# Sixteen-head attention: value projection one pair ahead, out projection begun at pair 6; latent attention's two value products together; squares of x through four banks

## The chip, the cores and the metric

One Trainium2 chip, one of its cores. The metric is the device time of one execution in microseconds (us), taken as the median of several runs. The five instruction queues of the core are TensorE (PE; its weight loads are PEld), VectorE (DVE), ScalarE (ACT), GpSimd (POOL) and SyncE (SP, which only issues loads here).

## What is computed

The reference is two transformer blocks on 512 tokens of width 1024, all in float32. Cut to what the change touches:

```python
# layer 0: latent attention, 8 heads of 128 + 64 rotary, values of 128
h = rms_norm(x, attn_pre_g[0]); a = h @ w_a; cq, ckv, kr = split(a)
q = rms_norm(cq, g_q) @ w_uq;   kv = rms_norm(ckv, g_kv) @ w_ukv
o = softmax(mask(q @ k.T * scale)) @ v;   x = x + rms_norm(o @ w_o, post_g)
x = x + rms_norm(swiglu(rms_norm(x, ffn_pre_g)), ffn_post_g)
# layer 1: attention of 16 heads of 64, with a relative bias table
k, v = rms_norm(x, g_src) @ w_kv;   q = rms_norm(x, attn_pre_g[1]) @ w_q
o = softmax(q @ k.T * 0.125 + bias) @ v;  x = x + rms_norm(o @ w_o, post_g)
...
# the second block (sparse attention, convolution, feed-forward) follows; the change does not touch it
```

## The kernel before

**Units of weights.** Every weight matrix is cut into units of 128 x 1024 values, 307 in all, consumed strictly in one order. Each goes through the same line: SP loads it into one of two `raw` buffers (`load_units`), ACT rounds it into a high part (`round_unit`, L380), POOL subtracts to get the low part (`low_units`, L385), and PE uses both (`next_unit` waits for the low part). One block of a product is three matmuls of 512 columns: high weight times high activation (L401), high times low (L402), low times high (L403); `project` does eight blocks, 24 matmuls, with one unit. Rounded units sit in two slots, `whi0/wlo0` and `whi1/wlo1`, taken in turn; a few units at stage borders have slots of their own (`OWN_AT`), numbered by distance from the first unit of a stage (`FIRST`). A slot is free when the projection that read it is done, and `round_unit` waits for that. Nothing schedules the queues: each engine's program is written out by hand, and the place of each `round_unit` call among ACT's other work is part of that text.

**The latent stage** (`latents_pe`, `latents_act`, `latents_dve`) projects x into five tiles (`("a", 0)` to `("a", 4)`), while ACT squares the eight tiles of x (`square_tile`, L517) through two banks of PSUM, and DVE adds them up (`add_square`, L1049), interleaved with the rotary tables (`dve_table`). PE sums over partitions inside projection 2 (`latent_sums_pe`) and spreads the inverse root inside projection 3 at block 2 (`spread_tokens_pe`, L1040).

**Latent attention** (`mla_pe`, `mla_act`, `mla_dve`) does four pairs of heads. At the end of pair p, PE does the value product of head 0 (`mla_times_v_pe`, L898), the two transposes of the next pair's values (`mla_values_pe`, L793), then the product of head 1.

**Attention of sixteen heads** (`b_pe`, `b_act`, `b_dve`) does eight pairs. For pair p+1 three units are needed, in the order v, k, q: units 92, 93, 94 for pair 0, 95, 96, 97 for pair 1, and so on to 115; units 116 to 123 are the out projection. The join before it (`b_first_pe`) already does v0, k0, q0, v1 and k1 (units 92 to 96). In pair p PE does the scores (`pair_scores_pe`, L1347), projects v and k of pair p+1, transposes the values (`b_values_pe`, L1403), transposes the probabilities (`pair_transposes_pe`, L1369), projects q of pair p+1, and does the value product (`pair_times_v_pe`, L1384). ACT, in pair p: the exponents (`act_exp`, L450), one `round_unit`, the copy of the values (`b_values_act`, L1408), six copies of transposed probabilities (`pair_spread_act`, L1377), two more `round_unit` (one in pair 0). DVE: the row minima of the scores (L1355), the scaling of projections (`dve_scale`, L514) and the normalising of the probabilities (`dve_normalise`, L456 and L465).

**The out projection** (`out_pe`, `out_act`, `out_dve`) is eight output tiles of eight blocks. Block k needs head pair k's output. Tile 0 is begun in the last pair, with seven of its blocks.

Of the kernel before, what the change touches and what calls it, by code (L numbers as in the profile page):

```python
# [12 lines left out]
P = 128  # L13
# [197 lines left out]
def build(nc, x_in, pos_in, stream, gains_in, consts_in, rel_in, w1_in, out):  # L211
# [115 lines left out]

    X_PIECES = (0, 1, 2, 4, 6)
    turn = {}
    FIRST = {"F0": 26, "B": 92, "F1": 124, "C": 190}  # L330
    OWN_AT = {"F0": (72, 80, 64), "B": (0, 8, 16), "F1": (48, 56, 36), "C": (0, 8, 16)}
    slot, before, last_in = [], [], {}
    for u in range(n_units):
        own = [(n, i) for n in FIRST for i, d in enumerate(((-4, 0), (-3, 1), (3,))) if u - FIRST[n] in d]
# [11 lines left out]
    def own_slot_free(e, u):  # L346

        for n, b in FIRST.items():
            i = {-4: 1, -3: 3, 3: 5}.get(u - b)
# [235 lines left out]

    def latent_sums_pe(e, name, key, src):
        e.wait_ge(*formed.at(key))
        token_sums_pe(e, R_BANK[name], src, True, True).then_inc(*summed.done((name, "tokens")))

    def latents_pe(e):  # L590
# [16 lines left out]
        project(e, 3, hh, hl, ("a", 3), between={2: lambda: spread_tokens_pe(e, 4, "x", 48)})  # L607
# [27 lines left out]
    def latents_act(e):  # L635
# [61 lines left out]
    def latents_dve(e):  # L697
# [9 lines left out]
        for k in range(1, KD):  # L707
            add_square(e, "x", k, bank[6:8])
# [202 lines left out]
    def mla_pe(e):  # L911
# [10 lines left out]
        for p in range(NA):  # L922
# [5 lines left out]
            else:  # L928
                u = next_unit(e)
                e.wait_ge(*low.at(("A", p - 1, 1)))  # L930
                out_blocks_pe(e, u, 0, (0, 1, 2))
# [8 lines left out]
            mla_times_v_pe(e, p, 0)  # L940
            if more:
                mla_values_pe(e, p + 1, 0)
                mla_values_pe(e, p + 1, 1)
            else:
                out_blocks_pe(e, u, 0, (5,))
            mla_times_v_pe(e, p, 1)
        return u

    def mla_act(e):
# [14 lines left out]
        for p in range(NA):  # L964
            more = p + 1 < NA
            if p:
                mla_out_act(e, p - 1, 1)
# [10 lines left out]
            mla_out_act(e, p, 0)  # L978
            if more:
                mla_values_act(e, p + 1)  # L980
        mla_out_act(e, NA - 1, 1)
# [98 lines left out]
    def out_pe(e, key, u, done):  # L1080

        last = ("A", NA - 1, 1) if key == "oA" else ("B", PAIRS_B - 1)
        us = (u, next_unit(e))
        out_blocks_pe(e, us[1], 1, (0, 1, 2))
        e.wait_ge(*low.at(last))
        for i, k in enumerate((done, 3)):
            out_blocks_pe(e, us[i], i, range(k, KD)).then_inc(*proj.done((key, i), ("unit", us[i])))
        for m in range(2, KD):
# [6 lines left out]
    def out_act(e, key):  # L1095
        for m in range(KD - 1):
            round_unit(e)
# [300 lines left out]

    def b_values_pe(e, p):

        e.wait_ge(*evicted.at(("vB", p) if p else ("kB", 1)))
        for t in range(QT):
            mm = e.transpose(bank[5 if p else 7][:, t * P:(t + 1) * P], vtmpB[:, t * P:(t + 1) * P], ident)  # L1403
# [759 lines left out]
```

## Time and profile before

| | |
|---|---|
| median of 3 runs | 1985.27 us (1985.1 to 1985.39) |
| the profiled execution, its own time | 1981.76 us |
| its span | 1980.0 us |
| PE busy | 1938.3 us, 98% of the span |
| POOL, ACT, DVE busy | 732.4, 722.6, 958.4 us |
| granted clock of TensorE, mean | 0.991 |

A busy share of 98% says that little can be won by making anything but PE wait less, and much can be lost by making PE wait. The timeline gives each instruction's start and length. Lengths of matmuls are modelled and overlap: successive matmuls of 512 columns start 0.23 us apart at full clock although each reads 0.39. So a stretch of PE's work is measured here from start to start.

### The profile page before, as it was taken

What the parts mean: (1) busy time and instruction counts of PE and PEld (TensorE: products, weight loads), DVE (VectorE), ACT (ScalarE), POOL (GpSimd) and SP (SyncE); (2) the same over time, 40 slices, a digit from 0 to 9 for tenths busy, and PEclk for the clock granted to TensorE, in tenths of its full rate; (3) what the DMA queues carried; (4) which work ended last, traced back from release to release, by engine and by line L of the source; (5) the groups of instructions that cost most, each with busy time, mean ns of one, the idle gap of its engine ahead of it and who ended that gap; (6) DMA issues with size and microseconds to landing.
All of it is one profiled execution on the core that took longest, in us unless ns stands there. A gap on an engine that the chain in (4) does not pass through costs nothing.

```text
span 1980.0 us, 22714 instructions
## 1 busy us (share of the span) xinstructions
PE 1938.3 (98%) x9094; PEld 1565.8 (79%) x9094; DVE 958.4 (48%) x1649; ACT 722.6 (36%) x1172; POOL 732.4 (37%) x309
## 2 busy tenths in 40 slices
PE   8999999999998999999999999899999999999998
PEld 7777888888886777888888888788677888888887
DVE  7563564441036445264444005894665765555202
ACT  6554422222244444332222224223654343333221
POOL 2333244444441222524444452342112444444442
PEclk9999999999999999999999999999899999999999
DMA  4412122332231222312233231321111222322222
GB/s 161 167 60 79 55 95 98 99 101 96 96 107 54 86 95 75 117 44 96 99 99 100 97 107 65 127 96 55 42 33 54 96 86 97 100 100 97 96 96 86
DMA packets 52152, 178.60 MB, mean 90 GB/s; under 512 B 5680, under 2 KB 5824, under 8 KB 51792
## 3 DMA queue, kind: packets, MB, share of 16 engines
q1 hardware_dynamic: 45776, 164.09, 25.1%
q10 hardware_dynamic: 6272, 13.07, 1.9%
q8 instruction: 72, 1.18, 0.2%
q14 instruction: 32, 0.26, 0.0%
HBM read 175.00 MB, written 6.33 MB: 92 GB/s over the span
## 4 chain that ended last, share of the span: by engine, by line
PE 87%; DVE 6%; ACT 3%; issue 2%; DMA 1%; POOL 1%; SPq 0%; DVEq 0%; ACTq 0%
PE bank L401 24%; PE bank L403 24%; PE bank L402 24%; PE bank L1384 2%; PE bank L1369 1%; PE bank L1137 1%; PE bank L1131 1%; PE bank L1132 1%; PE bank L1770 1%; PE bank L843 1%; PE bank L1347 1%; DVE tmp L1049 1%; PE bank L1040 1%; POOL wlo L385 1%; DMA raw<-stream 1%
## 5 line engine op out<-in xcount | busy, mean ns | idle before, releaser
L385 POOL TENSOR_TENSOR wlo<-raw,whi 128x1024 fp32r<-128x1024 f32 x285 | 684.6, 2403 | 1203.5 <-ACT whi L380 1203.4
L380 ACT ACTIVATE whi<-raw 128x1024 fp32r<-128x1024 f32 x287 | 304.1, 1060 | 851.6 <-PE bank L403 828.2
L401 PE MATMUL bank<-hh,whi 128*128 128x512 f32 x1384 | 545.1, 394 | 7.6 <-POOL wlo L385 6.3
L402 PE MATMUL bank<-hl,whi 128*128 128x512 f32 x1384 | 540.8, 391 | 0.0
L403 PE MATMUL bank<-hh,wlo 128*128 128x512 f32 x1384 | 540.7, 391 | 0.0
L401 PEld LDWEIGHTS bank<-hh,whi 128*128 128x128 f32 x1384 | 261.6, 189 | 71.4 <-issue 14.5
L403 PEld LDWEIGHTS bank<-hh,wlo 128*128 128x128 f32 x1384 | 261.1, 189 | 55.3
L402 PEld LDWEIGHTS bank<-hl,whi 128*128 128x128 f32 x1384 | 261.5, 189 | 53.2 <-issue 0.2
L514 DVE TENSOR_TENSOR tmp<-bank,rs 128x512 f32<-128x512 f32 x154 | 105.3, 689 | 237.8 <-PE bank L403 223.5
L401 PE MATMUL bank<-fh,whi 128*128 128x512 f32 x496 | 192.9, 389 | 0.0
L402 PE MATMUL bank<-fl,whi 128*128 128x512 f32 x496 | 192.9, 389 | 0.0
L403 PE MATMUL bank<-fh,wlo 128*128 128x512 f32 x496 | 192.9, 389 | 0.0
L1312 DVE TENSOR_TENSOR tmp<-tmp,tmp 128x512 f32<-128x512 f32 x44 | 99.0, 2249 | 49.9 <-ACT tmp L1267 49.5
L1326 DVE COPY y<-bank 128x512 f32<-128x512 f32 x16 | 11.0, 688 | 206.7 <-PE bank L403 206.7
L403 PEld LDWEIGHTS bank<-fh,wlo 128*128 128x128 f32 x496 | 93.1, 188 | 19.5
L402 PEld LDWEIGHTS bank<-fl,whi 128*128 128x128 f32 x496 | 93.1, 188 | 19.4
L401 PEld LDWEIGHTS bank<-fh,whi 128*128 128x128 f32 x496 | 93.1, 188 | 19.1
L1696 DVE SCALAR_TENSOR_TENSOR bank<-zpad,gn,bank 128x512 f32<-128x512 f32 x112 | 74.8, 749 | 0.0
L401 PE MATMUL bank<-oh,whi 128*128 128x512 f32 x160 | 63.7, 398 | 1.6 <-POOL wlo L385 1.5
L402 PE MATMUL bank<-ol,whi 128*128 128x512 f32 x160 | 62.3, 390 | 0.0
L403 PE MATMUL bank<-oh,wlo 128*128 128x512 f32 x160 | 62.3, 389 | 0.0
L1049 DVE TENSOR_TENSOR tmp<-tmp,bank 128x512 f32<-128x512 f32 x72 | 49.1, 683 | 24.9 <-ACT bank L517 23.5
(281 smaller groups left out, 2424.8 us busy)
## 6 DMA issues: line engine op xcount, KB each, us to landing
raw<-stream SPq DMA_DIRECT2D x307, 512.0 KB, 3.4
bias_scratch<-rel_scratch ACTq DMA_DIRECT2D x1, 4096.0 KB, 18.9
biasB<-bias_scratch ACTq DMA_DIRECT2D x16, 256.0 KB, 2.8
w<-w_in ACTq DMA_DIRECT2D x2, 1024.0 KB, 5.9
out<-y ACTq DMA_DIRECT2D x8, 256.0 KB, 2.1
x<-x_in SPq DMA_DIRECT2D x3, 512.0 KB, 8.9
x<-x_in SPq DMA_DIRECT2D x2, 256.0 KB, 5.5
cst<-consts_in SPq DMA_DIRECT2D x1, 448.0 KB, 4.3
```

The lines of the kernel that those rows point to most:

```text
L380: e.activation(slot[u][0][:, :], raw[u % 2][:, :], ACT.Copy).then_inc(*w_hi.done(u))
L385: e.tensor_tensor(slot[u][1][:, :], raw[u % 2][:, :], slot[u][0][:, :].bitcast(F32), ALU.subtract)\
L401: e.matmul(o, wh, h, start=first, stop=False)
L402: e.matmul(o, wh, l, start=False, stop=False)
L403: return e.matmul(o, wl, h, start=False, stop=last)
L514: e.tensor_tensor(dst, bank[bk][:, :], r[:, :], ALU.mult).then_inc(*evicted.done(key))
L843: e.matmul(bank[bk][:, c:c + W(t)], qn[b][h][:, t * P:(t + 1) * P], kn[b][h][:, 0:W(t)], start=False, stop=True, skip_group_check=True).th ...
L1040: mm = e.matmul(bank[bk][:, t * P:(t + 1) * P], stat[:, col + t:col + t + 1].to_broadcast([P, P]), ident, start=True, stop=True)
L1049: e.tensor_tensor(tmp[7][:, :], tmp[7][:, :], through[m % len(through)][:, :], ALU.add).then_inc(*formed.done((key, "sq", m)))
L1312: e.tensor_tensor(u[:, :], (bank[5] if conv else u)[:, :], g[:, :], ALU.mult).then_inc(*formed.done((key, "product", j)))
L1384: mm = e.matmul(bank[7][64 * h:64 * h + 64, k * P:T], vf(k, h), PTs[h][:, PT_AT[k]:PT_AT[k] + T - k * P], start=first and k == 0, stop=las ...
L1696: e.scalar_tensor_tensor(tmp[4][:, :] if tap == TAPS - 1 else s, zp[:, tap:tap + T], gg("dw", c * TAPS + tap), s, ALU.mult, ALU.add).then_ ...
```

## The change

It has five parts.

1. In pair p of the sixteen-head attention PE projects k and q of pair p+1 between the scores and the transposes, and v of pair **p+2** after the transposes (before: v and k, then q, all of pair p+1). In pair 0 it projects q1 there, transposes both v0 and v1, and projects v2 after. v1 is kept in `tmp7`. ACT's sequence in a pair is left as it was, but for the copies of pair 0 and one `round_unit` in pair 7, taken from the first tile of the out projection.
2. Pair 6 has no v to project, so it begins out tile 0 (five blocks); pair 7 does blocks 5 and 6 of it and seven blocks of tile 1; `out_pe` then begins tile 2. Three units are thus open together, and unit 118 gets its own slot.
3. Latent attention does both value products together, then the transposes of values.
4. Squares of x go through four banks instead of two.
5. The inverse root of x is spread at block 6 of projection 3 instead of block 2.

```diff
-    OWN_AT = {"F0": (72, 80, 64), "B": (0, 8, 16), "F1": (48, 56, 36), "C": (0, 8, 16)}
+    OWN_AT = {"F0": (72, 80, 64), "B": (0, 8, 16), "F1": (48, 56, 36, 40), "C": (0, 8, 16)}
...
+    X_THROUGH = (bank[6], bank[7], bank[3], bank[4])
...
-        project(e, 3, hh, hl, ("a", 3), between={2: lambda: spread_tokens_pe(e, 4, "x", 48)})
+        project(e, 3, hh, hl, ("a", 3), between={6: lambda: spread_tokens_pe(e, 4, "x", 48)})
...
-            square_tile(e, "x", k, x[:, k, :], bank[6:8])
+            square_tile(e, "x", k, x[:, k, :], X_THROUGH)
...
             mla_times_v_pe(e, p, 0)
+            if not more:
+                out_blocks_pe(e, u, 0, (5,))
+            mla_times_v_pe(e, p, 1)
             if more:
                 mla_values_pe(e, p + 1, 0)
                 mla_values_pe(e, p + 1, 1)
-            else:
-                out_blocks_pe(e, u, 0, (5,))
-            mla_times_v_pe(e, p, 1)
...
-    def out_pe(e, key, u, done):
...
+    def out_pe(e, key, begun, ahead):
+
+        n = len(begun)
+        u = next_unit(e)
+        out_blocks_pe(e, u, n, range(ahead))
+        e.wait_ge(*low.at(("A", NA - 1, 1) if key == "oA" else ("B", PAIRS_B - 1)))
+        for m, (um, done) in enumerate(begun + [(u, ahead)]):
+            out_blocks_pe(e, um, m, range(done, KD)).then_inc(*proj.done((key, m), ("unit", um)))
+        for m in range(n + 1, KD):
...
     def out_act(e, key):
         for m in range(KD - 1):
-            round_unit(e)
+            if m or key == "oA":
+                round_unit(e)
...
     def b_pe(e):
-            if more:
-                if p == 0:
-                    b_values_pe(e, 0)
-                else:
-                    project(e, 5, hh, hl, ("vB", p + 1))
-                if p:
-                    e.wait_ge(*stats.at(((("B", p), 1), "min", 1)))
-                    project(e, 6, hh, hl, ("kB", p + 1))
-                b_values_pe(e, p + 1)
+            if p == 0:
+                e.wait_ge(*evicted.at(("vB", 1)))
+                project(e, 5, h2h, h2l, ("qB", 1))
+                b_values_pe(e, 0)
+                e.wait_ge(*stats.at(((("B", 0), 1), "min", 1)))
+                b_values_pe(e, 1)
+                e.wait_ge(*spread.at(("vB", 0)))
+            elif more:
+                e.wait_ge(*evicted.at(("vB", p + 1)))
+                project(e, 5, hh, hl, ("kB", p + 1))
+                e.wait_ge(*stats.at(((("B", p), 1), "min", 1)))
+                project(e, 6, h2h, h2l, ("qB", p + 1))
+                e.wait_ge(*evicted.at(("kB", p + 1)))
+                b_values_pe(e, p + 1)
             else:
-                u = next_unit(e)
                 e.wait_ge(*low.at(("B", p - 1)))
-                out_blocks_pe(e, u, 0, range(6))
+                out_blocks_pe(e, u, 0, (5, 6))
+                e.wait_ge(*stats.at(((("B", p), 1), "min", 1)))
+                u1 = next_unit(e)
+                out_blocks_pe(e, u1, 1, range(4))
...
             pair_transposes_pe(e, ("B", p), probsB)
             if more:
-                e.wait_ge(*spread.at(("vB", p + 1)))
-                project(e, 5, h2h, h2l, ("qB", p + 1))
+                e.wait_ge(*(spread.at(("vB", p + 1)) if p else evicted.at(("qB", 1))))
+            if p + 2 < PAIRS_B:
+                project(e, 5, hh, hl, ("vB", p + 2))
+            elif more:
+                u = next_unit(e)
+                out_blocks_pe(e, u, 0, range(5))
             else:
-                out_blocks_pe(e, u, 0, (6,))
+                out_blocks_pe(e, u1, 1, (4, 5, 6))
...
     def b_act(e):
             if more:
                 load_bias(e, p + 1, 0)
                 load_bias(e, p + 1, 1)
-                round_unit(e)
+            round_unit(e)
+            if p == 0:
+                b_values_act(e, 0)
+            if more:
                 b_values_act(e, p + 1)
...
     def b_dve(e):
-            if more:
-                e.wait_ge(*proj.at(("vB", p + 1)))
-                if p == 0:
-                    e.wait_ge(*turned.at(("vB", 0)))
-                dve_scale(e, 5, rs[0], vtmpB[:, :], ("vB", p + 1))
+            if p and more:
+                e.wait_ge(*proj.at(("kB", p + 1)))
+                dve_scale(e, 5, rs[0], kB[nb][:, :], ("kB", p + 1))
...
```

The first place is PE in pair 1 of the sixteen-head attention, from its first projection to its value product. `whi0` and `whi1` are the two slots, `hh` the activation for k and v, `h2h` that for q; the other 23 matmuls of each projection are left out. Before:

```order
L1347 MATMUL bank3<-kB1_93,qB1_91 128x512
L401 MATMUL bank5<-hh_50,whi0_54 128x512 [waits weight_low]
L401 MATMUL bank6<-hh_50,whi1_55 128x512 [waits weight_low,statistic]
L1403 MATMUL bank5<-cst_135,vtmpB_100 128x128 [waits evicted]
L1369 MATMUL bank0<-cst_135,probsB0_96 128x128 [waits statistic,normalised,low_part]
L401 MATMUL bank5<-h2h_88,whi0_54 128x512 [waits weight_low,transposed_copied]
L1384 MATMUL bank7<-PTB0_98,vB1_95 64x512 [waits transposed_copied]
```

and in the changed kernel:

```order
L1350 MATMUL bank3<-kB1_93,qB1_91 128x512
L402 MATMUL bank5<-hh_50,whi1_55 128x512 [waits weight_low,evicted]
L402 MATMUL bank6<-h2h_88,whi0_54 128x512 [waits weight_low,statistic]
L1412 MATMUL bank5<-cst_135,vtmpB_100 128x128 [waits evicted]
L1372 MATMUL bank0<-cst_135,probsB0_96 128x128 [waits statistic,normalised,low_part]
L402 MATMUL bank5<-hh_50,whi1_55 128x512 [waits weight_low,transposed_copied]
L1387 MATMUL bank7<-PTB0_98,vB1_95 64x512 [waits transposed_copied]
```

The three projections were units 98, 99 and 100 (slots 0, 1, 0) and are now units 99, 100 and 101 (slots 1, 0, 1): one unit further in the stream, at the same three places.

The second place is ACT in the same pair 1, in the changed kernel, from the last exponent on (L451) through the two bias loads, three roundings (L381), the copy of values (L1417) and the copies of probabilities (L1380):

```order
L451 ACTIVATE probsB1_97,stat_142<-probsB1_97,stat_142 128x512 [waits statistic]
L1400 DMA biasB0_101<-bias_scratch 128x512 [waits statistic]
L1400 DMA biasB1_102<-bias_scratch 128x512 [waits statistic]
L381 ACTIVATE whi0_54<-raw0_52 128x1024 [waits projected,raw_loaded0]
L1417 ACTIVATE vB0_94<-bank5 128x512 [waits transposed]
L1380 ACTIVATE PTB0_98<-bank0 128x512 [waits transposed,mixed]
L1380 ACTIVATE PTB1_99<-bank2 128x512 [waits transposed]
L1380 ACTIVATE PTB1_99<-bank3 128x512 [waits transposed]
L1380 ACTIVATE PTB1_99<-bank7 128x256 [waits transposed]
L381 ACTIVATE whi1_55<-raw1_53 128x1024 [waits projected,raw_loaded1]
L381 ACTIVATE whi0_54<-raw0_52 128x1024 [waits projected,raw_loaded0]
```

Before, the rows are the same, in the same order (with L450, L1397, L380, L1408 and L1377 as their lines): the roundings of pair 1 are units 100, 101 and 102 in both kernels. Nothing moved here while PE moved.

The third place is PE at the end of pair 0 of latent attention (L898 the value products, L793 the transposes of values). Before:

```order
L898 MATMUL bank7<-PTB0_98,vA00_80 128x128
L793 MATMUL bank6<-cst_135,vtmpB_100 128x128 [waits evicted]
L793 MATMUL bank5<-cst_135,tmp7_131 128x128 [waits evicted]
L898 MATMUL bank1<-PTB1_99,vA01_81 128x512 [waits transposed_copied]
L898 MATMUL bank1<-PTB1_99,vA01_81 128x128
```

and in the changed kernel:

```order
L901 MATMUL bank7<-PTB0_98,vA00_80 128x128
L901 MATMUL bank1<-PTB1_99,vA01_81 128x512 [waits transposed_copied]
L901 MATMUL bank1<-PTB1_99,vA01_81 128x128
L796 MATMUL bank6<-cst_135,vtmpB_100 128x128 [waits evicted]
L796 MATMUL bank5<-cst_135,tmp7_131 128x128 [waits evicted]
```

The product of head 1 now stands between the product of head 0 and the wait for the evicted values.

## Rows read from the trace of the kernel before

**Rows 1.** Busy time by engine, then clock, DMA share, GB/s: pair 0; pairs 1 to 6.
```profile
616.00:638.00 22.00, 15.84 (x85) 10.78 (x85) 10.78 (x31) 11.43 (x27) 3.03 (x2) 0.92 0.17 61
638.00:781.00 143.00, 143.00 (x770) 109.72 (x768) 71.30 (x198) 64.08 (x156) 43.14 (x19) 1.00 0.27 89
```

**Rows 2.** Timeline of PE, pair 1: start us, length us, engine, line, what.
```profile
638.32 2.43 PE L1347 MATMUL bank<-kB,qB 64*128 64x128 f32 x16
640.68 0.50 PE L401 MATMUL bank<-hh,whi 128*128 128x512 f32 x1
...
652.13 2.35 PE L1369 MATMUL bank<-cst,probsB 128*128 128x128 f32 x20
654.24 0.48 PE L401 MATMUL bank<-h2h,whi 128*128 128x512 f32 x1
```

**Rows 3.** Timeline of ACT, pair 1: last exponent's sum, roundings, copies of probabilities.
```profile
644.70 0.19 ACT L450 ACTIVATION_READ_ACCUMULATOR probsB<-probsB,stat 128x1 f32 x1
646.51 1.06 ACT L380 ACTIVATE whi<-raw 128x1024 fp32r<-128x1024 f32 x1 [1.63 <-PE bank L403]
...
652.83 2.62 ACT L1377 ACTIVATE PTB<-bank 128x512 f32<-128x512 f32 x6
655.28 1.10 ACT L380 ACTIVATE whi<-raw 128x1024 fp32r<-128x1024 f32 x1
```

**Rows 4.** Timeline of ACT, POOL and PE: one unit from rounding to first use.
```profile
797.11 1.06 ACT L380 ACTIVATE whi<-raw 128x1024 fp32r<-128x1024 f32 x1 [5.51 <-PE bank L403]
...
798.25 2.40 POOL L385 TENSOR_TENSOR wlo<-raw,whi 128x1024 fp32r<-128x1024 f32 x1 [15.42 <-ACT whi L380]
...
800.70 0.50 PE L401 MATMUL bank<-oh,whi 128*128 128x512 f32 x1 [0.29 <-POOL wlo L385]
```

**Rows 5.** Granted clock (third number from the end) after PE's longest wait, 5.50 us.
```profile
1256.00:1258.00 2.00, 1.73 (x4) 1.47 (x5) 2.00 (x5) 0.00 (x0) 0.13 (x1) 0.50 0.44 86
1258.00:1260.00 2.00, 2.00 (x7) 1.56 (x7) 2.00 (x5) 0.69 (x2) 0.00 (x0) 0.67 0.46 184
```

**Rows 6.** Timeline of PE, pair 0, from the scores' end to the projection of q1.
```profile
618.86 0.66 PE L1403 MATMUL bank<-cst,vtmpB 128*128 128x128 f32 x4
622.18 0.66 PE L1403 MATMUL bank<-cst,vtmpB 128*128 128x128 f32 x4 [2.67 <-DVE vtmpB L514]
...
629.65 0.99 PE L1369 MATMUL bank<-cst,probsB 128*128 128x128 f32 x7 [1.84 <-DVE probsB L465]
630.39 0.48 PE L401 MATMUL bank<-h2h,whi 128*128 128x512 f32 x1
```

**Rows 7.** Timeline of DVE and POOL, pair 1: two normalisings and a low part.
```profile
647.26 3.41 DVE L465 TENSOR_SCALAR probsB<-probsB,stat 128x128 f32<-128x128 f32 x4
...
650.80 1.28 DVE L465 TENSOR_SCALAR probsB<-probsB,stat 128x128 f32<-128x128 f32 x4
...
647.65 2.48 POOL L385 TENSOR_TENSOR wlo<-raw,whi 128x1024 fp32r<-128x1024 f32 x1 [7.98 <-ACT whi L380]
```

**Rows 8.** Timeline of PE, end of pair 1 of latent attention.
```profile
117.38 0.66 PE L793 MATMUL bank<-cst,vtmpB 128*128 128x128 f32 x4 [0.75 <-DVE vtmpB L514]
...
118.47 2.32 PE L898 MATMUL bank<-PTB,vA 128*128 128x512 f32 x8
120.72 1.14 PE L838 MATMUL bank<-krope,qr 64*128 64x128 f32 x8
```

**Rows 9.** Timeline of PE and ACT, latent stage: two waits, unit 5's rounding, projection 4.
```profile
28.12 0.50 PE L401 MATMUL bank<-hh,whi 128*128 128x512 f32 x1 [0.81 <-POOL wlo L385]
...
37.83 1.16 PE L1040 MATMUL bank<-cst,stat 128*128 128x128 f32 x8 [1.69 <-DVE stat L695]
...
42.92 0.39 PE L401 MATMUL bank<-hh,whi 128*128 128x512 f32 x1
...
37.47 1.04 ACT L380 ACTIVATE whi<-raw 128x1024 fp32r<-128x1024 f32 x1
```

**Rows 10.** Timeline of DVE, pair 7: sum of the minimum that frees bank 6.
```profile
786.05 0.08 DVE L1355 DVE_READ_ACCUMULATOR2_ANT stat<- 128x1 f32 x1
```

More of the change, by code:

```diff
@@ L330, in build @@
     FIRST = {"F0": 26, "B": 92, "F1": 124, "C": 190}
-    OWN_AT = {"F0": (72, 80, 64), "B": (0, 8, 16), "F1": (48, 56, 36), "C": (0, 8, 16)}
+    OWN_AT = {"F0": (72, 80, 64), "B": (0, 8, 16), "F1": (48, 56, 36, 40), "C": (0, 8, 16)}
     slot, before, last_in = [], [], {}
     for u in range(n_units):
-        own = [(n, i) for n in FIRST for i, d in enumerate(((-4, 0), (-3, 1), (3,))) if u - FIRST[n] in d]
+        own = [(n, i) for n in FIRST for i, d in zip(range(len(OWN_AT[n])), ((-4, 0), (-3, 1), (3,), (-6,))) if u - FIRST[n] in d]
         if own:
@@ L707, in latents_dve @@
         for k in range(1, KD):
-            add_square(e, "x", k, bank[6:8])
+            add_square(e, "x", k, X_THROUGH)
             dve_table(e, next(tables))
@@ L930, in mla_pe @@
                 e.wait_ge(*low.at(("A", p - 1, 1)))
+                e.wait_ge(*spread.at(("v1", p)))
                 out_blocks_pe(e, u, 0, (0, 1, 2))
@@ L1397, in load_bias, with values_of @@
         e.dma_start(biasB[h][:, :], bias_dram[2 * p + h, :, :]).then_inc(*bias_got[h].done(p))
+    VALUES_IN = (7, 6) + (5,) * (PAIRS_B - 2)
+    def values_of(p):
+        return tmp[7] if p == 1 else vtmpB
     def b_values_pe(e, p):
-        e.wait_ge(*evicted.at(("vB", p) if p else ("kB", 1)))
+        e.wait_ge(*evicted.at(("vB", p)))
         for t in range(QT):
-            mm = e.transpose(bank[5 if p else 7][:, t * P:(t + 1) * P], vtmpB[:, t * P:(t + 1) * P], ident)
+            mm = e.transpose(bank[VALUES_IN[p]][:, t * P:(t + 1) * P], values_of(p)[:, t * P:(t + 1) * P], ident)
         mm.then_inc(*turned.done(("vB", p)))
@@ L1407, in b_values_act @@
         e.wait_ge(*turned.at(("vB", p)))
-        e.activation(vB[p % 2][:, :, :], bank[5 if p else 7][:, :].rearrange("p (k c) -> p k c", c=P), ACT.Copy).then_inc(*spread.done(("vB", p)))
+        e.activation(vB[p % 2][:, :, :], bank[VALUES_IN[p]][:, :].rearrange("p (k c) -> p k c", c=P), ACT.Copy).then_inc(*spread.done(("vB", p)))
     def b_mins_dve(e, p, h):
@@ L1501, in b_dve @@
             if more:
-                if p:
-                    e.wait_ge(*proj.at(("kB", p + 1)))
-                    dve_scale(e, 6, rs[0], kB[nb][:, :], ("kB", p + 1))
                 e.wait_ge(*proj.at(("qB", p + 1)))
-                dve_scale(e, 5, rs[0], qB[nb][:, :], ("qB", p + 1))
+                dve_scale(e, 6 if p else 5, rs[0], qB[nb][:, :], ("qB", p + 1))
+            if p + 2 < PAIRS_B:
+                e.wait_ge(*proj.at(("vB", p + 2)))
+                e.wait_ge(*turned.at(("vB", p + 1 if p else 0)))
+                dve_scale(e, 5, rs[0], vtmpB[:, :], ("vB", p + 2))
             e.wait_ge(*mixed.at(("B", p)))
```

23 lines of the change are left out of this document (7 added, 16 removed).

## The prediction

> **What bounds the kernel now.** I read the busy times by stage first. PE is the bound, and in pairs 1 to 6 of the sixteen-head attention it never rests: 143.00 us busy in 143.00 [rows 1]. Only pair 0 shows holes, 15.84 busy in 22.00. Then I read PE's timeline there, for what ends its waits, and beside it ACT's, since every projection needs a weight unit that ACT rounds and POOL completes. In pair 1 the scores start at 638.32; call that S. The first projection starts at S + 2.36, and the transposes run from 652.13 (S + 13.81) to 654.24 [rows 2]. ACT ends its exponents at about 644.79 (S + 6.47) and its copies of probabilities at 655.28, where the next rounding starts [rows 3]. The rounding at 646.51 waited for PE to free the slot, not PE for it: weights are early. From the start of a rounding to PE's first matmul with that unit is 800.70 - 797.11 = 3.59 us [rows 4]. A projection takes 24 matmuls of 0.227, 5.45 us: 630.39 + 5.45 is pair 0's product, and the two projections of pair 1 fit between 640.68 and 652.13 (2 x 5.45, plus 0.45 for the transposes of values, leaves next to nothing).
>
> **The change, part by part.** The sum is made against the profiled execution, 1981.76 us; the median of the runs, 1985.27, lies 3.5 above it, and I carry that offset over.
>
> *Pairs 1 to 6: the weights come late.* Nothing is added to PE's work: the same three projections stand at the same three places of a pair. But each uses the unit one further on, while ACT rounds the units where it did. Before, pair 1 used units 98, 99, 100; now 99, 100, 101, and ACT rounds 100 after the exponents and 101 after the copies of probabilities.
> - Unit 100, for q2, is wanted at S + 2.36 + 5.45 = S + 7.81. ACT is in its exponents until S + 6.47, so PE can start at S + 6.47 + 3.59 = S + 10.06 [rows 3, 4]. PE waits 2.25. Before, the unit in this place had been rounded in the pair before.
> - Unit 101, for v3, is wanted when the transposes are done, 2.11 after their start [rows 2]. ACT rounds it behind six copies, which themselves need the transposes; that rounding starts 655.28 - 652.13 = 3.15 after their start, and PE can use it 3.59 later, at 6.74 [rows 2 to 4]. PE waits 4.63. No slack elsewhere shortens this: transposes, copies, rounding, low part, projection are now one chain.
>
> Behind these waits on PE stand the value product and the next pair's scores, and DVE and ACT wait for those, so the pair gets longer by 6.9. In pair 6 the third user is out tile 0 (unit 116), with the same wait. Six pairs: 6 x 6.88 = **+41.3**. The bias loads, the raw loads and the second rounding at the pair's end keep their slack: unit 102 is done some 2.4 after unit 101, long before its use.
>
> *The clock.* In pairs 1 to 6 it is 1.00 now, 2.4 GHz [rows 1]. No row shows a wait of 4.6 that recurs. The nearest are the 5.50 us wait, after which the clock was 0.50, then 0.67 of full (1.2 GHz, then back), a loss of 0.5 x 1.73 + 0.33 x 2 = 1.5 us [rows 5], and pair 0, whose waits of 2.67 and 1.59 bring the mean of 22 us to 0.92 [rows 1, 6]. So a wait of 4.6 costs between 0 and 1.5; it is nearest to the 5.50, but part of the slow time may fall into the wait, so I take 1.2, six times: **+7.2** (0 to 9). For the wait of 2.25, nearer to the 1.84 of pair 0, I take 0 (0 to 9 for six).
> The Trainium skill's page TensorE: Matmul & The Clock Gate ("HAM oscillation — how this bites in real kernels") says that recurring waits between bursts throttle the array again every time, so that each burst starts cold. That speaks against this change; by it all twelve waits would pay, a rival below.
>
> *Pair 0.* From the end of the scores to the projection of q1 are 630.39 - 618.86 = 11.5 us, for 3.1 us of transposes: 8.4 of waiting [rows 6]. Now q1's projection fills the first 5.45 (unit 97 is ready), the values take 0.9, and the probabilities should be turned by about 628. Why 628: DVE scales v1 before the minima, which makes them 0.2 later than in pair 1 relative to the scores, so the exponents end near 616.5 + 6.7 = 623.2 and the second head is normalised between 625 and 627.5. The projection of v2 follows at 628 where q1's began at 630.39, with 5.45 more already done: 2.4 + 5.45 = **-7.8** (-6 to -8.4). That the second normalising may take 3.4 instead of 1.3 is the spread: one beside a low part on POOL took 3.41, one alone 1.28 [rows 7].
> The Trainium skill's SBUF — State Buffer ("Who interferes with whom") calls the port pair that DVE and GpSimd share an exclusive lock; the trace agrees. In pairs 1 to 6 that lengthens the first normalising too, but it ends by S + 11.5 and the transposes now start at S + 16, so it costs nothing there.
>
> *Pair 7 and the out projection.* PE does the same 24 + 24 + 24 matmuls of tiles 0 to 2. New is a wait for bank 6: the minimum is read at 786.05, 4.6 after that pair's scores, and blocks 5 and 6 end at 2.36 + 1.36 = 3.7, so 0.9 is lost [rows 10]. Gone are the 0.29 wait of the third tile for POOL and about a microsecond of small gaps, since more work stands between a slot's release and its next use [rows 4]: **-0.4** (-1.0 to +1.5, the latter if unit 118's low part holds up DVE).
>
> *Latent attention.* PE waits 0.75 for evicted values before their transposes, in three pairs [rows 8]. Now the product of head 1, 120.72 - 118.47 = 2.25, stands in that wait; the copies it needs are done before. Next late is the values' copy on ACT, needed only in the second half of the scores, 3 us on. 3 x 0.73 = **-2.2** (-1.5 to -2.4).
>
> *Latent stage.* With four banks ACT's squares no longer wait for DVE, so unit 3 is rounded when its slot is free and the 0.81 wait goes. The spread at block 6 comes 12 matmuls, 2.7 us, later, so its 1.69 wait goes [rows 9]. That is 2.5 at most. What is late next is unit 5 for projection 4: it is rounded at 37.47, behind the cosine and the root on ACT, which move by 0.4 at most; 37.1 + 3.59 = 40.7 against 42.92 before gives **-2.2** (-1.0 to -2.5).
>
> Sum: 41.3 + 7.2 - 7.8 - 0.4 - 2.2 - 2.2 = **+35.9**, so 1981.76 + 35.9 = 2017.7 for a profiled execution, and **2021** for the median. Least: 41.3 - 8.4 - 1.0 - 2.4 - 2.5 = +27. Most: 41.3 + 9 + 9 - 6 + 1.5 - 1.5 - 1.0 = +52.
>
> **The rivals.**
> - *A. The weights are in time; faster.* The five savings then stand alone: -12.6, 1972.7. It needs unit 100 by S + 7.8 and unit 101 by the end of the transposes, that is roundings that start by S + 4.2 and before the copies. For it speaks that every rounding in pairs 1 to 6 had to wait for a slot, not for ACT, or came early. Against it, ACT runs in written order and that order did not move. It decides from a rounding 2.3 and 4.6 earlier than I find.
> - *B. Only one of the two waits bites*, the second: +41.3 falls by 13.5, giving 2007.7. For it: the first is only 2.25, and exponents that ended 2 us sooner would hide it. Against: they are tied to the scores through DVE, unchanged.
> - *C. The clock never falls*: +35.9 - 7.2 = +28.7, 2014. For it: the waits are shorter than the 5.50.
> - *D. It falls after both waits* of each pair: +35.9 + 9 + 1.8, 2032.
>
> **How the numbers follow.** Forecast 0.60, A 0.05, B 0.07, C 0.15, D 0.11, and 0.02 for a change that moves nothing measurable. The forecast's own spread is about 5 to each side; 2008 to 2033 takes in C and D and about half of B, and leaves out A. A measurement of this kernel can tell 0.2%, 4 us, from no change. Faster by more than that only in A: 0.05; same 0.02; slower 0.93.
>
> **What would show it.** PE busy falls to about 112 in 143 us of pairs 1 to 6, a pair takes 31 to 32 us instead of 143.00 / 6 = 23.8, and the first matmul of a projection waits for POOL's low part some 12 times, 2.2 and 4.6 us long. ACT's roundings no longer wait for PE there. The clock shows about six short drops. In pair 0 the wait for the values is gone; in latent attention the 0.75 waits are gone; the spread of x's root waits for nothing. I am wrong if the low parts are there before PE asks, or if a pair still takes 24 us.

## The result: slower by 2.4%, and the profile after

The changed kernel takes 2032.12 us (median of 6 runs, 2029.99 to 2032.76). The kernel before takes 1984.35 us (median of 6 runs, 1982.75 to 1985.39). The ratio is 1.024, with a 95% interval of 1.0226 to 1.0253. The prediction was 2021 us in a range of 2008 to 2033, with 0.93 on slower: the direction and the range hold, and the time is 11 us above the forecast. It comes within 1 us of the range's upper end, and it falls on the number of rival D, 2032.

The profiled execution of the changed kernel has a span of 2031.0 us, 51.0 more than before. Its page, first the busy times, then the group of the first matmuls of a projection block with its idle time:

```profile
span 2031.0 us, 22734 instructions
...
PE 1955.8 (96%) x9094; PEld 1577.7 (78%) x9094; DVE 952.0 (47%) x1649; ACT 720.5 (35%) x1172; POOL 731.4 (36%) x309
...
L402 PE MATMUL bank<-hh,whi 128*128 128x512 f32 x1384 | 549.4, 397 | 29.0 <-POOL wlo L386 27.8
```

The same number of matmuls, 9094, keeps PE busy 17.5 us longer than before (1938.3). Where the granted clock reads 0.50, as after the wait of 4.47 in pair 1, a matmul of 512 columns has a length of 0.63 us in place of 0.39; that is what makes the busy time grow. The other 33.5 us of the 51 are idle time. The row of the page is for the activation `hh` alone; the view of PE's waits takes all of them together (total, times, longest):

```profile
PE bank L402 <- POOL wlo L386: 46.3, 16, 5.5
```

Before, that wait was 7.8 us in 5 times. Twelve of the 16 stand in pairs 1 to 6 and make 38.8 of the 46.3. By stretch (pair 0, then pairs 1 to 6 and half a pair around them; columns as in [rows 1]):

```profile
613.00:632.00 19.00, 18.75 (x106) 14.02 (x106) 11.16 (x32) 10.17 (x26) 4.76 (x2) 1.00 0.29 94
638.00:781.00 143.00, 115.14 (x536) 86.09 (x535) 46.75 (x143) 43.88 (x109) 30.45 (x13) 0.90 0.21 67
```

Against [rows 1], pair 0 has lost its holes (before, 15.84 busy in 22.00 us at a clock of 0.92). The 143 us in which PE never rested now have 115 busy, at a mean clock of 0.90, and 536 records in place of 770.

PE's timeline of pair 1 answers to [rows 2] and shows both waits. Here S, the start of the scores, is 632.58:

```profile
632.58 2.43 PE L1350 MATMUL bank<-kB,qB 64*128 64x128 f32 x16
...
642.67 0.47 PE L402 MATMUL bank<-h2h,whi 128*128 128x512 f32 x1 [2.00 <-POOL wlo L386]
648.65 2.35 PE L1372 MATMUL bank<-cst,probsB 128*128 128x128 f32 x20
655.46 0.77 PE L402 MATMUL bank<-hh,whi 128*128 128x512 f32 x1 [4.47 <-POOL wlo L386]
663.87 2.37 PE L1387 MATMUL bank<-PTB,vB 128*64 128x512 f32 x16
666.18 2.00 PE L1350 MATMUL bank<-kB,qB 64*128 64x128 f32 x14
```

Unit 100 is used at S + 10.09; the prediction had S + 10.06. Unit 101 is used 655.46 - 648.65 = 6.81 after the transposes start; the prediction had 6.74. ACT's and POOL's timelines show the two chains:

```profile
638.95 0.19 ACT L451 ACTIVATION_READ_ACCUMULATOR probsB<-probsB,stat 128x1 f32 x1
639.05 1.04 ACT L381 ACTIVATE whi<-raw 128x1024 fp32r<-128x1024 f32 x1
...
649.34 2.62 ACT L1380 ACTIVATE PTB<-bank 128x512 f32<-128x512 f32 x6
651.79 2.04 ACT L381 ACTIVATE whi<-raw 128x1024 fp32r<-128x1024 f32 x2
```

```profile
640.17 2.35 POOL L386 TENSOR_TENSOR wlo<-raw,whi 128x1024 fp32r<-128x1024 f32 x1 [10.99 <-ACT whi L381]
652.97 4.68 POOL L386 TENSOR_TENSOR wlo<-raw,whi 128x1024 fp32r<-128x1024 f32 x2 [10.45 <-ACT whi L381]
```

ACT begins the rounding of unit 100 right behind its last exponent, POOL follows, and PE waits for both. ACT no longer waits for PE there, as it did at 646.51 before [rows 3]: the slot is free and the rounding is what is late. All six pairs have the same two waits, 2.00 and 4.47.

The starts of the scores give the length of each pair. Before, each pair took 23.86 us. Now pairs 1 to 5 take 33.60, 32.27, 34.02, 34.05 and 34.04. Pair 6 takes 31.99, with 15 matmuls (3.4 us) where a projection (5.45 us) stood, so 34.04 for equal work. The waits alone make 30.74, as experiment 2 shows. The rest is the clock. Three stretches of the changed kernel (third number from the end): after the 4.47 wait of pair 1, after the 2.00 wait of pair 2 and after the 2.00 wait of pair 4:

```profile
654.00:656.00 2.00, 0.54 (x1) 0.50 (x2) 0.00 (x0) 0.00 (x0) 2.00 (x2) 0.65 0.00 0
656.00:658.00 2.00, 2.00 (x6) 1.58 (x5) 0.00 (x0) 0.00 (x0) 1.65 (x1) 0.50 0.74 250
...
676.00:678.00 2.00, 1.73 (x8) 1.47 (x9) 1.97 (x8) 0.00 (x0) 0.12 (x1) 1.00 0.38 84
678.00:680.00 2.00, 2.00 (x11) 1.65 (x10) 0.59 (x2) 0.00 (x0) 0.00 (x0) 1.00 0.46 178
...
742.00:744.00 2.00, 1.44 (x5) 1.25 (x6) 1.97 (x7) 0.00 (x0) 0.41 (x1) 0.84 0.34 49
744.00:746.00 2.00, 2.00 (x6) 1.51 (x6) 0.88 (x3) 0.00 (x0) 0.00 (x0) 0.50 0.54 213
```

At 0.50 (1.2 GHz) a window of 2 us counts 6 matmuls, at 1.00 (2.4 GHz) 11. The clock fell after all six waits of 4.47 and after four of the six waits of 2.00, those of pairs 3 to 6: ten times. In pairs 3 to 6 both falls together cost 34.04 - 30.74 = 3.3 us. In pairs 1 and 2 the one fall, after the 4.47, cost 2.86 and 1.53.

### The profile page after: what moved, and what is told of

Same layout as the page of the kernel before. It is cut to its first block, busy times and chain, and to the rows that moved or that the text cites. A ratio compares the mean times of both kernels' runs of the same rounds, so it can differ in the third digit from the quotient of the medians.

```text
span 2031.0 us, 22734 instructions
## 1 busy us (share of the span) xinstructions
PE 1955.8 (96%) x9094; PEld 1577.7 (78%) x9094; DVE 952.0 (47%) x1649; ACT 720.5 (35%) x1172; POOL 731.4 (36%) x309
## 4 chain that ended last, share of the span: by engine, by line
PE 84%; DVE 6%; ACT 5%; POOL 2%; issue 2%; DMA 1%; SPq 0%; ACTq 0%; DVEq 0%
PE bank L402 24%; PE bank L403 23%; PE bank L404 23%; POOL wlo L386 2%; PE bank L1387 2%; ACT probsB L451 1%; ACT whi L381 1%; PE bank L1140 1%; PE bank L1134 1%; PE bank L1135 1%; PE bank L1792 1%; PE bank L846 1%; PE bank L901 1%; DVE tmp L1051 1%; PE bank L1042 1%
## 5 line engine op out<-in xcount | busy, mean ns | idle before, releaser
L381 ACT ACTIVATE whi<-raw 128x1024 fp32r<-128x1024 f32 x286 | 302.3, 1061 | 809.0 <-PE bank L404 784.9
L451 ACT ACTIVATE probsB<-probsB,stat 128x128 f32<-128x128 f32 (+1 forms) x64 | 35.2, 552 | 90.8 <-DVE stat L1358 90.8
L386 POOL TENSOR_TENSOR own_lo<-raw,own_hi 128x1024 fp32r<-128x1024 f32 x21 | 50.2, 2391 | 34.4 <-ACT own_hi L381 34.3
```

The lines of the kernel that those rows point to most:

```text
L381: e.activation(slot[u][0][:, :], raw[u % 2][:, :], ACT.Copy).then_inc(*w_hi.done(u))
L386: e.tensor_tensor(slot[u][1][:, :], raw[u % 2][:, :], slot[u][0][:, :].bitcast(F32), ALU.subtract)\
L451: e.activation(r, r, ACT.Exp, scale=-1.0, bias=stat[:, st + t:st + t + 1], accum_out=stat[:, st + 4 + t:st + 5 + t]).then_inc(*expd.done(( ...
```

## The experiments

Theory: PE waits only because it uses each unit one place further on while ACT rounds where it did, and each wait brings its own fall of the clock. The rivals are given with each run.

**1. ACT one unit ahead as well.**

```diff
             if more:
                 load_bias(e, p + 1, 0)
                 load_bias(e, p + 1, 1)
-            round_unit(e)
+            if more:
+                round_unit(e)
...
             if more:
                 round_unit(e)
-                if p:
-                    round_unit(e)
+                round_unit(e)
```

> The changed kernel with one rounding of a weight unit moved on ACT: from pair 7 of the sixteen-head attention to the end of pair 0, so that ACT, too, is one unit further in pairs 1 to 6. My theory (PE waits in pairs 1 to 6 only because its projections use the unit one further on while ACT rounds as before): no wait of PE for POOL's low part is left in pairs 1 to 6, the clock stays at full there, a pair takes about 23.9 us again, and the whole time falls by about 60 us against the changed kernel, to 1970 to 1975 us, which is also 10 us under the kernel before. Rival 1 (the order of the projections itself, or the value product behind it, makes the pair longer): pairs stay over 30 us and the time stays above 2015. Rival 2 (the rounding that comes earlier at the end of pair 0 only moves the wait, because its slot is not free): waits of 2 to 5 us with the releaser ACT or POOL remain in each pair, time between 1985 and 2020.

Measured: 1971.85 us (1970.68 to 1973.04), ratio to the kernel before 0.9936 (0.9923 to 0.995). In pairs 1 to 6 no wait of PE is left in the trace. Pairs 1 to 5 take 23.86 us each, as before. From the windows view of this run, 640 to 780 us:

```profile
640.00:780.00 140.00, 139.31 (x752) 106.28 (x751) 71.97 (x203) 63.99 (x156) 43.29 (x18) 1.00 0.27 88
```

ACT's timeline of this run, at the end of pair 0, behind pair 1's exponents and behind pair 1's copies:

```profile
625.24 1.10 ACT L381 ACTIVATE whi<-raw 128x1024 fp32r<-128x1024 f32 x1
630.07 1.06 ACT L381 ACTIVATE whi<-raw 128x1024 fp32r<-128x1024 f32 x1 [3.73 <-PE bank L404]
...
640.39 1.06 ACT L381 ACTIVATE whi<-raw 128x1024 fp32r<-128x1024 f32 x1 [1.63 <-PE bank L404]
...
649.16 1.10 ACT L381 ACTIVATE whi<-raw 128x1024 fp32r<-128x1024 f32 x1
```

The row at 640.39 again waits 1.63 for PE, exactly as in [rows 3]. One `round_unit` moved 60 us (2032.1 - 1971.9). The order of the projections on PE costs nothing by itself, and both named rivals fall.

**2. The waits kept, the clock held up.**

```diff
                 e.wait_ge(*stats.at(((("B", p), 1), "min", 1)))
+                fill_clock(e, 7, 6)
                 project(e, 6, h2h, h2l, ("qB", p + 1))
...
+            if p and more:
+                fill_clock(e, 17, 5)
             if p + 2 < PAIRS_B:
                 project(e, 5, hh, hl, ("vB", p + 2))
```

> The changed kernel with matmuls that keep TensorE at work during its two waits for weights in pairs 1 to 6: 7 matmuls of 512 columns of constants (1.6 us) into bank 6 ahead of the projection of q, and 17 (3.9 us) into bank 5 ahead of the third projection; both banks are overwritten by what follows, and the results are unchanged. This parts the cost of the waits from that of the clock. Theory (each of the two waits is followed by a drop of the granted clock to half that costs about 1.65 us; 11 drops between 654 and 826 us of the changed kernel): the first matmul of each projection comes no earlier, but the clock stays at 1.00, a pair takes 23.86 + 2.0 + 4.5 + 0.3 = 30.7 us instead of 34.0, and the time is about 18 us under the changed kernel, near 2014. Rival 1 (the pair is 34 us long because of the waits and something that follows from them other than the clock, such as DVE or ACT being late): the clock stays full but the pair stays over 33 us, less than 5 us won. Rival 2 (the matmuls that fill come too late or end too late and only add to the wait): pairs of 34 to 36 us with a full clock.

The filling matmuls are of 128 columns in float32, which the trace shows as two matmuls each, not of 512 as the expectation says; their time, 1.72 and 3.96 us, is close to what is stated there. Measured: 2012.16 us (2011.39 to 2012.33), 20.0 under the changed kernel. PE's timeline in pair 1 of this run:

```profile
638.34 1.72 PE L1029 MATMUL bank<-cst 128*128 128x128 f32 x14
640.42 0.50 PE L402 MATMUL bank<-h2h,whi 128*128 128x512 f32 x1 [0.35 <-POOL wlo L386]
646.45 2.35 PE L1372 MATMUL bank<-cst,probsB 128*128 128x128 f32 x20
648.63 3.96 PE L1029 MATMUL bank<-cst 128*128 128x128 f32 x34
653.18 0.50 PE L402 MATMUL bank<-hh,whi 128*128 128x512 f32 x1 [0.59 <-POOL wlo L386]
```

The third projection again starts 653.18 - 646.45 = 6.73 after the transposes, so the weights come as late as before, but the clock is 1.00 over 140 us:

```profile
640.00:780.00 140.00, 134.35 (x800) 108.63 (x800) 46.96 (x142) 46.91 (x113) 33.33 (x15) 1.00 0.21 68
```

Pairs 1 to 4 take 30.74 to 30.76 us; pair 5 takes 31.64, because its first wait is 0.9 longer (1.27). Rivals 1 and 2 fall. So the two waits cost 30.74 - 23.86 = 6.88 us a pair, the prediction's figure, and what is above 30.74 in the changed kernel is the clock (above 28.69, this run's figure, in pair 6). Pair by pair that is 2.86, 1.53, 3.28, 3.31, 3.30 and 3.30: 17.6 us. In this run itself the pairs win 16.7, since pair 5 loses 0.9 of it again to its longer wait. The rest of the 20.0 comes from elsewhere: pair 0 begins 2.2 us earlier (611.05 for 613.22), and the stages behind pair 7, which the edit does not touch, are 1.9 us shorter.

**3. Only the first wait left.**

```diff
             round_unit(e)
+            if p and more:
+                round_unit(e)
...
             if more:
                 round_unit(e)
-                if p:
-                    round_unit(e)
```

> The changed kernel with the roundings of ACT in another place: in pairs 1 to 6 two units are rounded right after the exponents and one at the pair's end (before: one and two). The second wait (4.47 us, for the unit rounded behind six copies) should be gone, the first (2.00 us) stay. It tells what each wait costs by itself. Theory (price of the first wait 2.2 us plus its own drop of the clock, 1.65 us): a pair takes 23.9 + 2.2 + 1.65 = 27.7 us, the time is about 39 us under the changed kernel, near 1993. Rival 1 (the 2.00 wait alone does not lower the clock, as after it in pairs 1 and 2; it fell in later pairs only since both waits lie close together): pairs of 26.1, clock full, near 1983. Rival 2 (the copies of probabilities, which now stand behind two roundings, the second of which waits for PE to free the slot, become late and hold up the value product): the 4.47 wait is replaced by another behind the copies, pairs over 29 us.

Measured: 1991.65 us (1990.48 to 1993.92), ratio 1.0035 (1.0023 to 1.0047). The 4.47 waits are gone and six of 2.01 stay. Pairs 1 to 5 take 26.16, 27.74, 26.16, 27.71 and 27.72 us. Theory and rival 1 are each right in some of the pairs: without a fall the wait costs 26.16 - 23.86 = 2.30, and three of the six pairs pay some 1.55 more for one. Rival 2 falls: nothing took the place of the second wait. Two of these waits, in pairs 3 and 4 of this run, and the granted clock around them:

```profile
695.26 0.47 PE L402 MATMUL bank<-h2h,whi 128*128 128x512 f32 x1 [2.01 <-POOL wlo L386]
...
721.42 0.47 PE L402 MATMUL bank<-h2h,whi 128*128 128x512 f32 x1 [2.01 <-POOL wlo L386]
```

```profile
694.00:696.00 2.00, 0.74 (x3) 0.67 (x4) 1.97 (x3) 0.41 (x1) 2.00 (x2) 1.00 0.00 0
696.00:698.00 2.00, 2.00 (x10) 1.62 (x9) 2.00 (x3) 0.00 (x0) 1.47 (x1) 1.00 0.78 260
...
720.00:722.00 2.00, 0.58 (x3) 0.53 (x4) 1.97 (x4) 0.56 (x1) 2.00 (x2) 1.00 0.00 0
722.00:724.00 2.00, 2.00 (x7) 1.52 (x6) 2.00 (x2) 0.00 (x0) 1.61 (x1) 0.53 0.81 225
```

The waits are alike and PE does the same work around them, yet the clock stays at 1.00 after the one and falls after the other. A wait of 2 us may lower the clock or not, and these rows do not tell which.

**4. Only the second wait left empty.** The edit is the first hunk of experiment 2 alone.

> The changed kernel with constant matmuls (7 of 128 columns in float32, 1.7 us in the trace of the run that filled both waits) only ahead of the projection of q, in the first wait of pairs 1 to 6; the second wait, 4.47 us, stays empty. Results are unchanged. This is the case on which the prediction's clock term was built: both waits cost their time, and the clock falls after the second alone. Theory (each wait has its own drop, about 1.65 us): the drops after the first wait are gone, six after the second stay, a pair is 34.0 - 1.65 = 32.4 us, the time 2021 to 2024. Rival 1 (the drop after the second wait comes only because the first has already left TensorE idle: with the first filled the clock stays full throughout): pairs 30.9, time near 2013. Rival 2 (filling the first moves the drop, which comes anyway once in a pair and then lasts longer): pairs 33.5 to 34, 2029 to 2032.

Measured: 2026.2 us (2024.23 to 2030.38), ratio 1.021 (1.0193 to 1.0228), a little above the theory's 2021 to 2024. The clock no longer falls after the first wait, so each of those falls belongs to its own wait. Rival 1 falls. But the six falls after the second wait cost more than I expected of them. Pairs 1 to 5 take 33.06, 33.51, 32.25, 33.14 and 33.58 us, which is 2.32, 2.77, 1.51, 2.40 and 2.84 above 30.74; pair 6, at 30.20, is 1.51 above its 28.69 in experiment 2. Together 13.4 us, in place of 6 x 1.65 = 9.9. Rival 2 is thus partly right: in four of the pairs the clock stays low for longer. Pair 1 of the changed kernel already was such a case: its wait of 2.00 left the clock at full, and the one fall after the 4.47 cost 2.86. From the windows view of pair 1 in this run:

```profile
652.00:654.00 2.00, 0.00 (x0) 0.00 (x0) 0.00 (x0) 0.86 (x1) 2.00 (x1) 0.61 0.00 0
654.00:656.00 2.00, 1.52 (x4) 1.27 (x5) 0.00 (x0) 0.00 (x0) 2.00 (x2) 0.50 0.34 63
656.00:658.00 2.00, 2.00 (x6) 1.57 (x5) 0.00 (x0) 0.00 (x0) 0.66 (x1) 0.50 0.68 229
658.00:660.00 2.00, 2.00 (x7) 1.56 (x6) 0.00 (x0) 0.00 (x0) 0.00 (x0) 0.68 0.64 238
```

The clock is down already during the wait, and is still down 4 us after it.

**5 to 7. The latent parts on the kernel before.** Experiment 5 takes parts 3 to 5 of the change, experiment 6 part 3 alone, experiment 7 parts 4 and 5 alone. Part 3 comes with a change on ACT: the copy of head 1's output now stands behind that of head 0 and no longer in the next pair. The core of the three:

```diff
             mla_times_v_pe(e, p, 0)
+            mla_times_v_pe(e, p, 1)
             if more:
                 mla_values_pe(e, p + 1, 0)
                 mla_values_pe(e, p + 1, 1)
...
-            square_tile(e, "x", k, x[:, k, :], bank[6:8])
+            square_tile(e, "x", k, x[:, k, :], X_THROUGH)
...
-        project(e, 3, hh, hl, ("a", 3), between={2: lambda: spread_tokens_pe(e, 4, "x", 48)})
+        project(e, 3, hh, hl, ("a", 3), between={6: lambda: spread_tokens_pe(e, 4, "x", 48)})
```

> The kernel before with only the latent parts of the change: squares of x through four banks, the spread of x's inverse root at block 6, and both value products of latent attention together. The sixteen-head attention is as it was. The prediction's sum gives -2.2 for the latent stage and -2.2 for latent attention, so 1980.9 for the median. The trace of the changed kernel shows -1.84 and -3.3 for these stages, which gives 1980.1 if nothing is lost behind them; but that trace kept only 3.3 of these 5.1 by the scores of pair 0, because the clock fell for longer at 572.5 us. If such a loss comes with any shift of the start of that stage, this kernel is at 1981 to 1982; if it was chance, at 1979.5 to 1980.5. Rival: the stages behind wait for something else than PE and take the gain back, no difference (1984 to 1985).

Measured: 1978.58 us (1976.96 to 1981.39), ratio 0.9971 (0.996 to 0.9981), 6.0 us less by the medians, on the stages' 5.1. The gain is kept. This is shorter than both ranges of the expectation, and on the side of chance. The six profiled executions that run the same program up to pair 0 (the changed kernel and experiments 1 to 4 and 8) start it anywhere from 611.05 to 614.71, so the 1.9 us that the changed kernel seemed to lose there are no more than they differ by among themselves.

> The kernel before with only the latent attention of the change (both value products, then the transposes of the next values). The prediction gave -2.2 (three waits of 0.73); the traces of the changed kernel and of the run with all latent parts show -1.1 for each of three pairs, -3.3. Theory (the wait that goes is 0.75, and a further 0.35 a pair goes with the gaps around it): 3.3 less than before in the trace at the out projection, a median near 1981. Rival (the stages behind take it back, or the clock's drop near 580 us gets longer by as much): 1983 to 1984.5.

Measured: 1980.84 us (1976.91 to 1985.18), ratio 0.9983 (0.9974 to 0.9993), 3.6 us less by the medians, near the theory's 3.3. PE's timeline, end of pair 1 of latent attention in this run, which answers to [rows 8]:

```profile
114.20 4.47 PE L898 MATMUL bank<-PTB,vA 128*128 128x512 f32 x16
118.51 0.60 PE L793 MATMUL bank<-cst,vtmpB 128*128 128x128 f32 x4
...
119.48 1.14 PE L838 MATMUL bank<-krope,qr 64*128 64x128 f32 x8
```

From the first value product to the next scores it is 119.48 - 114.20 = 5.28 us. Before, it was 120.72 - 114.31 = 6.41. The recorded wait was 0.75; what went is 1.1.

> The kernel before with only the latent stage of the change (squares of x through four banks, the spread of the inverse root at block 6 of projection 3). The prediction gave -2.2 (-1.0 to -2.5); the trace of the changed kernel has -1.84 at the scores of latent attention. Theory: -1.8 in the trace at 66 us and a median near 1982.5, ratio 0.999. Rival (the earlier start is lost again at the borders of the following stages, where a wait is set by loads or by the clock): no difference.

Measured: 1982.43 us (1978.41 to 1985.89), ratio 0.9988 (0.9977 to 0.9999), 2.0 us less by the medians. The interval just leaves out 1. The trace has -2.19 at the start of latent attention's scores (63.70 for 65.89). That is one execution against one: in experiment 6, whose latent stage is the old one, these scores start at 66.91, 1.0 later than before, after a clock of 0.83 in the stretch from 12 to 20 us, where the kernel before has 1.00. The two waits of [rows 9] are gone; one of 0.3 is new, of the sums over partitions for DVE's addition of squares:

```profile
29.01 1.05 PE L1034 MATMUL bank<-cst,tmp 128*128 128x1 f32 x8 [0.28 <-DVE tmp L1051]
```

**8. A version that beats both kernels.** Experiment 1, and unit 119 rounded ahead of the square of out tile 0.

```diff
     def out_act(e, key):
         for m in range(KD - 1):
-            if m or key == "oA":
-                round_unit(e)
-            if m in (1, 2, 3):
+            round_unit(e)
+            if m in (1, 2, 3) and (key == "oA" or m > 1):
                 round_unit(e)
```

> The changed kernel with the rounding moved from pair 7 to the end of pair 0 (as in the first experiment, which gave 1971.9 and a ratio of 0.9936) and, in the out projection, unit 119 rounded ahead of the square of tile 0 instead of behind it. In that first experiment PE still waited 0.78 us for this unit at 795.41. Theory (the wait is there because the rounding stands behind a square that waits for tile 0): it goes, 0.8 us less, near 1971.1, ratio 0.9932; that is at the limit of what can be told, so the trace decides. Rival (the square comes late and the mean over the tiles with it, or the slot is not free earlier): the same 0.8 or more is lost at the next tile.

Measured: 1967.32 us (1966.95 to 1973.03), ratio 0.9918 (0.9904 to 0.9932). It is 0.8% faster than the kernel before and 3.2% faster than the changed one. Against experiment 1 the medians differ by more than the wait that was removed, but the intervals overlap, and the profiled execution here is the slowest of the six (1973.03). The stage itself decides: the trace says that the wait is gone and nothing took its place. From the start of pair 7's scores to the sums over the tiles it is 48.80 us, and 49.91 in experiment 1. ACT's timeline of this run, with the rounding now ahead of the square:

```profile
792.51 1.06 ACT L381 ACTIVATE whi<-raw 128x1024 fp32r<-128x1024 f32 x1 [6.44 <-PE bank L404]
793.48 0.62 ACT L518 ACTIVATE tmp<-y 128x512 f32<-128x512 f32 x1
```

## Why the prediction was right, and where it was 11 us short

- **The sum: predicted +35.9, measured +51.0 between the profiled executions.** For the changed kernel's profiled execution the sum gave 2017.7, and it took 2032.76: 15.1 short. The median is only 11 short because the forecast carried over the 3.5 us by which the profiled execution before lay under its median, while the changed kernel's lies 0.6 above its own. These 4.2 us are luck.
- **The two waits: predicted +41.3, measured +41.3.** Experiment 2 has them without the clock, 6.88 us a pair. That the figure fits so exactly is in part luck: by experiment 3 the first wait cost 2.30 (2.25 in the prediction), which leaves 4.58 for the second (4.63). The view that gave this was the timeline of ACT held against PE's start of scores: two chains, each of one rounding, one low part and one projection.
- **The clock: predicted +7.2, measured +17.6. This is the step that failed**: "so I take 1.2, six times" for the wait of 4.6, and 0 for the wait of 2.25. Experiment 3 shows that a 2.0 wait alone lowers the clock in some pairs, at about 1.55 us each time; in the changed kernel it did so in four of six. Experiment 4 shows that the fall after the second wait alone costs 1.5 to 2.8, 13.4 us in six, so that even in the forecast's own case the term was half its size. The bound of 9 for the wait of 4.6 did not hold either: it is passed by that 13.4, and by the changed kernel's own share of some 11.4 (an estimate, 17.6 less 4 x 1.55 for the short waits). Only both bounds together, 18, took the 17.6 in.

  The row I took as the nearest for the short wait, the 1.84 in pair 0 [rows 6], had shown only the mean of a stretch with several waits in it, and that mean, 0.92, was itself the sign of a fall.

  Of the rivals, D is nearest to what happened; 0.11 was too little for it. Its own case did not quite come true: it has twelve falls of 1.5, and there were ten, one of them of 2.86. And its 2032 holds the 3.5 carried over; for the profiled execution it gives 2028.5, 4.3 under the 2032.76. The signs named for the forecast's case say the same: pairs of 31 to 32 us and about six short drops were expected, and there are pairs of up to 34 and ten drops.

  The Trainium skill's page TensorE: Matmul & The Clock Gate ("HAM oscillation — how this bites in real kernels") tells of a kernel whose waits for DMA, some 3 to 5 us each, throttle the array again every time. The prediction took that for all twelve waits here; the page's case is like the waits of 4.47 alone, and these agree with it, six of six. The waits of 2.00 are shorter than any it tells of, and they lowered the clock in four of six; experiment 3 has two like ones with different outcomes.
- **Pair 0: predicted -7.8, measured -7.9.** It takes 632.58 - 613.22 = 19.36 us in place of 21.82, with 5.45 more of projection in it. PE's timeline there, which answers to [rows 6]:

```profile
621.17 0.60 PE L1412 MATMUL bank<-cst,vtmpB 128*128 128x128 f32 x4
...
622.46 2.40 PE L1372 MATMUL bank<-cst,probsB 128*128 128x128 f32 x20 [0.25 <-ACT vB L1417]
624.62 0.47 PE L402 MATMUL bank<-hh,whi 128*128 128x512 f32 x1
```

- **Pair 7 and the out projection: predicted -0.4, measured +2.4.** From pair 7's scores to the sums over the tiles it is 884.02 - 832.55 = 51.47 us; before, it was 833.92 - 781.48 = 52.44, with 15 matmuls, 3.4 us, more to do. The 2.4 lie outside the term's bounds (-1.0 to +1.5). Three waits make it. The one for bank 6 was foreseen at 0.9 and is 0.68. The second, 1.38, is what the upper bound was for: unit 118's low part on POOL runs beside a normalising on DVE, which then takes 3.41 us where the one just before took 1.27. DVE's, POOL's and PE's timelines:

```profile
837.93 1.27 DVE L466 TENSOR_SCALAR probsB<-probsB,stat 128x128 f32<-128x128 f32 x4
...
839.61 3.41 DVE L466 TENSOR_SCALAR probsB<-probsB,stat 128x128 f32<-128x128 f32 x4
```

```profile
840.39 2.35 POOL L386 TENSOR_TENSOR own_lo<-raw,own_hi 128x1024 fp32r<-128x1024 f32 x1 [13.16 <-ACT own_hi L381]
```

```profile
843.08 0.98 PE L1372 MATMUL bank<-cst,probsB 128*128 128x128 f32 x7 [1.38 <-DVE probsB L466]
...
856.24 0.50 PE L402 MATMUL bank<-oh,whi 128*128 128x512 f32 x1 [0.79 <-POOL wlo L386]
```

In experiment 1 that low part comes earlier, the two normalisings take 1.28 and 1.27, and the wait is gone. The Trainium skill's SBUF — State Buffer ("Who interferes with whom") has the port pair of these two engines as an exclusive lock, which these rows agree with. The third wait, 0.79 for unit 119, I had missed. The rounding taken out of tile 0 of the out projection left unit 119's rounding behind a square that waits for that tile. Experiment 8 shows it by moving it.
- **Latent attention: predicted -2.2, measured -3.3; latent stage: predicted -2.2, measured -1.8** (-2.2 in experiment 7, against a kernel before whose start of these scores can differ by 1.0 between executions). The sum was right to 0.7. The mechanism holds in both. In latent attention a recorded wait was worth more than its length; in the latent stage the wait of 0.3 for DVE is what I had not seen as late next.
- **Not in the sum at all**: between latent attention and pair 0 the clock stayed low for longer than before at 572 us, and 1.9 of the 5.1 us won were gone by pair 0. The later stages, behind the sums over the tiles, add 0.9. Executions of the same program differ by as much in both places (experiments 5 and 2), so the runs do not show either to be an effect of the change. For the later stages it stays open: the eight profiled executions with the new latent stage take 1145.1 to 1147.2 us there, the two with the old one 1146.1 and 1143.5, too few to tell. The terms then close: -1.8 - 3.3 + 1.9 - 7.9 + 41.3 + 17.6 + 2.4 + 0.9 = 51.1, and the spans differ by 51.0.
- **Rival A**, weights in time, was priced at 1972.7. Experiment 1 is that case, made by one moved rounding, and it measures 1971.85: the savings together were priced right, and only the place of ACT's roundings kept them from showing.

What stays open: what decides whether a wait of 2 us lowers the clock, and why it stays low for longer in some pairs of experiment 4 than in others. The runs count these cases and price them, but don't explain them.

## What to carry to other kernels

When a consumer is moved one step ahead in a stream of prepared operands, every engine that prepares them has to be moved by the same step; otherwise each step of the loop pays the distance. Write down for one turn of the loop when each operand is wanted and when its preparation can start; here that gave the cost of a pair, 6.88 us, and the cure, one rounding moved from the last pair to the end of pair 0. Where a change makes TensorE wait regularly, add a clock term for every wait, the short ones too: 1.5 us each was the least that any fall cost here, against waits of 2.3 and 4.6.

## What the runs showed of the hardware

- Equal waits of 2.01 us on PE, with equal work around them, were followed by a clock of 1.00 in one pair and 0.53 in the next (experiment 3); in all, after 7 of 12 such waits in two kernels the clock fell. A fall cost 1.5 to 1.6 us after such a wait, and 1.5 to 2.9 after a wait of 4.47.
- A wait on PE costs more than the trace records as idle. The recorded 2.00 cost 2.30, the 4.47 cost 4.58, and taking out a recorded 0.75 won 1.1. Some 0.16 of the difference is the modelled end of the matmul ahead (0.39 long at a pace of 0.23); the rest wasn't looked into.
- Constant matmuls of 1.72 and 3.96 us in two waits of a pair kept the clock at 1.00 over 140 us and won 16.7 us in these six pairs, without any weight coming sooner (experiment 2).
